# Banded attention by key groups, with the last two query tiles of its input product set between its first eight units

## What is computed

```python
def cd_mixer(u, w_in, w_out, conv_w, conv_b, w_a, b_a, w_x, b_x, lam, sinks):
    c_x, c_gate, d_q, d_k, d_v = _split(u @ w_in, CD_SIZES)      # 512, 512, 512, 128, 128 columns
    y_c = rg_lru_block(c_x, c_gate, conv_w, conv_b, w_a, b_a, w_x, b_x, lam)
    y_d = swa_sink_attention(d_q.reshape(bn, s_len, D_HEADS, D_HEAD_DIM), ...)
    return jnp.concatenate([y_c, y_d], axis=-1) @ w_out

def swa_sink_attention(q, k, v, sinks):      # 8 heads of 64, 2 key heads, 4 heads each
    ...
    s = jnp.einsum('bnqkgd,bnskd->bnkgqs', qc, kb).astype(F32) * (dh ** -0.5)
    s = jnp.where(valid[None, :, None, None, None, :], s, -jnp.inf)
    sink = ...
    p = jax.nn.softmax(jnp.concatenate([s, sink], axis=-1), axis=-1)[..., :-1]
    o = jnp.einsum('bnkgqs,bnskd->bnqkgd', p.astype(vb.dtype), vb)
```

## Time and profile before

| | |
|---|---|
| median of 3 runs | 2368.01 us (2366.35 to 2370.50) |
| the profiled execution | 2372.35 us, its span 2370.6 us |
| mean granted clock of TensorE | 0.992 of full |
| PE busy | 2324.5 us, 98% |
| DVE, ACT, POOL busy | 1646.2, 1026.0, 550.0 us (69%, 43%, 23%) |
| the chain that ended last | PE 90%, DVE 5%, ACT 3%, issue 1% |

### The profile page before, as it was taken

One profiled execution on the slowest core, in us unless ns is written; L12 is line 12 of the kernel. 1 busy time (PEld: TensorE's weight loads), 2 busy tenths in 40 slices (PEclk: granted clock), 3 DMA queues, 4 the chain that ended last, 5 costly groups with the idle time before them and its releaser, 6 DMA issues.

```text
span 2370.6 us, 33754 instructions
## 1 busy us (share of the span) xinstructions
PE 2324.5 (98%) x12906; PEld 1833.7 (77%) x12906; DVE 1646.2 (69%) x2657; ACT 1026.0 (43%) x1815; POOL 550.0 (23%) x510
## 2 busy tenths in 40 slices
PE   9999999999999999999999999989999999999998
PEld 6587778865587888888888867867878888888887
DVE  5388787887657977777655587456588677765557
ACT  5333335756634433333333444466343333333344
POOL 5025544323100243333320000000014333341000
PEclk9999999999999999999999999989999999999999
DMA  6121100010043455545696521101335445468663
GB/s 179 54 71 54 45 28 21 3 37 1 28 151 137 138 163 176 169 151 178 209 306 193 186 70 45 45 28 55 123 116 195 160 160 178 149 205 301 205 192 129
DMA packets 236271, 298.26 MB, mean 126 GB/s; under 512 B 13424, under 2 KB 175232, under 8 KB 227024
## 3 DMA queue, kind: packets, MB, share of 16 engines
q1 hardware_dynamic: 220848, 207.66, 28.4%
q0 software_dynamic: 15264, 88.45, 10.0%
HBM read 206.95 MB, written 88.60 MB: 125 GB/s over the span
## 4 chain that ended last, share of the span: by engine, by line
PE 90%; DVE 5%; ACT 3%; issue 1%; POOL 0%; DVEq 0%; ACTq 0%; POOLq 0%
PE ps L378 26%; PE ps L380 25%; PE ps L379 25%; PE ps L3228 2%; PE ps L3216 1%; PE ps L3248 1%; ACT d_p L1723 1%; PE ps L2555 1%; PE ps L2024 1%; DVE met L2326 1%; PE ps L2569 1%; PE ps L2564 1%; PE ps L1978 1%; PE ps L1537 1%; PE ps L2606 0%
## 5 line engine op out<-in xcount | busy, mean ns | idle before, releaser
L378 PE MATMUL ps<-uhi,whi 128*128 128x512 f32 x608 | 246.9, 406 | 7.6 <-DVE ulo L537 3.4
L378 PE MATMUL ps<-q_T,whi 128*128 128x512 f32 x640 | 249.1, 389 | 1.6 <-ACT upr L862 1.6
L380 PE MATMUL ps<-q_T,wlo 128*128 128x512 f32 x640 | 249.0, 389 | 0.0
L379 PE MATMUL ps<-q_T,whi 128*128 128x512 f32 x640 | 249.0, 389 | 0.0
L378 PE MATMUL ps<-q_B,whi 128*128 128x512 f32 x608 | 238.9, 393 | 2.4 <-DVE q_B L537 2.4
L378 PE MATMUL ps<-ahi,whi 128*128 128x512 f32 x616 | 240.4, 390 | 0.0
L380 PE MATMUL ps<-ahi,wlo 128*128 128x512 f32 x616 | 239.7, 389 | 0.0
L379 PE MATMUL ps<-alo,whi 128*128 128x512 f32 x616 | 239.7, 389 | 0.0
L380 PE MATMUL ps<-uhi,wlo 128*128 128x512 f32 x608 | 237.1, 390 | 0.0
L379 PE MATMUL ps<-ulo,whi 128*128 128x512 f32 x608 | 237.0, 390 | 0.0
L380 PE MATMUL ps<-q_B,wlo 128*128 128x512 f32 x608 | 236.7, 389 | 0.0
(11 more groups left out here) (485 smaller groups left out, 5001.4 us busy)
## 6 DMA issues: line engine op xcount, KB each, us to landing
wraw<-in_ffn_w_gate_dram SPq DMA_DIRECT2D x44, 512.0 KB, 5.5
wd<-in_ffn_w_down_dram POOLq DMA_DIRECT2D x22, 1024.0 KB, 7.3
w_sums<-wd POOLq DMA_DIRECT2D x22, 1024.0 KB, 4.9
wraw<-w_sums SPq DMA_DIRECT2D x40, 512.0 KB, 3.8
araw<-act_sums SPq DMA_DIRECT2D x40, 512.0 KB, 4.7
wraw<-in_ffn_w_down_dram SPq DMA_DIRECT2D x30, 512.0 KB, 5.9
araw<-acts SPq DMA_DIRECT2D x30, 512.0 KB, 6.7
wraw<-in_ab_w_in_dram SPq DMA_DIRECT2D x24, 512.0 KB, 3.8
```

The source lines that it names most:

```text
L378: nc.tensor.matmul(dst, wh, xh, start=start, stop=False, **kw)
L379: nc.tensor.matmul(dst, wh, xl, start=False, stop=False, **kw)
L380: return nc.tensor.matmul(dst, wl, xh, start=False, stop=stop, **kw)
```

## The change

The tiles are multiplied in another order: query tiles 0 and 1, keys, values, and then query tiles 2 and 3 (12 and 13 in the list). These two are no longer whole products ahead of the attention. Their 32 steps (three matmuls each: one channel piece, one half of the rows) are issued by `late_queries(pe, first_, end)` at given places: four before the transposes of the value tile, four after them, and 24 between the units 0 to 6. They use bank 0 for the first half of the rows and bank 1 for the second; `late_move(act, m)` copies each finished half (four copies of 512 columns in place of two of 1024).

The units go by groups: n is group n // 8, block n % 8, so that the first eight need query tiles 0 and 1 alone. The first eight share one pair of score banks (2 and 3), since 0 and 1 hold the late product: `scores(n + 1)` comes one unit ahead and waits for `bias(n)`. From unit 8 on the order is as before. The second weight tile of the output product is split inside the attention (ACT at n = 3, DVE at n = 4). `vrow`, `d_s`, `d_pt` and `d_p` have new places, since `uhi` and `ulo` are still read; POOL clears the first 64 columns of each `d_p` after `dk` is there.

```diff
-    order += [("cd", DQ0 + P * j) for j in range(6)]
+    order += [("cd", DQ0 + P * j) for j in (0, 1, 4, 5, 2, 3)]
...
-            for i in range(10, 13):
+            for i in range(10, 12):
                 pe.wait_ge(*after("dq_moved", i - 9))
                 gemm(pe, t[i], pair(i % 2), *u)
-            pe.wait_ge(*after("dq_moved", 4))
-            gemm(pe, t[13], pair(1), *u)
+            late_queries(pe, 0, 4)
             pe.wait_ge(*after("dv_copied", 1))
             for b in range(NB):
                 last = pe.transpose(pair(1)[:, b * P:(b + 1) * P], tmp[0][:, b * P:(b + 1) * P], ident[:, :])
             last.then_inc(S("dv_turned"), 1)
+            late_queries(pe, 4, 8)
+
+        def late_queries(pe, first_, end):
+
+            for s in range(first_, end):
+                i, h, k = 12 + s // 16, s // 8 % 2, s % 8
+                t = Tile(n_cd + i)
+                if s % 16 == 0:
+                    w_ready(pe, t)
+                if s == 0:
+                    pe.wait_ge(*after("dk_moved", 1))
+                if s in (16, 24):
+                    pe.wait_ge(*after("dq_moved", 3 + h))
+                last = three_pass(bank(h), whi[:, t.slot, k * P:(k + 1) * P], wlo[:, t.slot, k * P:(k + 1) * P],
+                                  uhi[:, k, rows_of(h)], ulo[:, k, rows_of(h)], k == 0, k == KT - 1)
+                if k == KT - 1:
+                    last.then_inc(S("w_used") if h else after("d_half", 0)[0], 1)
+
+        def late_move(act, m):
+
+            i, h = divmod(m, 2)
+            if h:
+                tile_done(act, Tile(n_cd + 12 + i))
+            else:
+                act.wait_ge(*after("d_half", i + 1))
+            act.activation(dq[:, 2 + i, rows_of(h)], bank(h), ACT.Copy).then_inc(S("dq_moved"), 1)
...
+        def d_bank(n):
+
+            return 2 if n < NB else 2 * (n % 2)
+
         def swa_pe(pe):
             def scores(n):
-                b, g = divmod(n, 2)
-                if n >= 2:
-                    pe.wait_ge(*after("d_biased", n - 1))
+                g, b = divmod(n, NB)
+                if n == NB:
+                    pe.wait_ge(*after("dq_moved", 6))
+                elif n:
+                    pe.wait_ge(*after("d_biased", n if n < NB else n - 1))
...
             scores(0)
-            scores(1)
-            for n in range(2 * NB):
+            ends = (8, 12, 16, 19, 23, 26, 29, 32)
+            for n in range(NB - 1):
+                scores(n + 1)
+                middle = ends[n + 1] if n == NB - 2 else ends[n] + 2
+                late_queries(pe, ends[n], middle)
+                turn(n)
+                late_queries(pe, middle, ends[n + 1])
+                if n:
+                    values(n - 1)
+            scores(NB)
+            for n in range(NB - 1, 2 * NB):
                 if n + 2 < 2 * NB:
                     scores(n + 2)
                 turn(n)
-                if n:
-                    values(n - 1)
+                values(n - 1)
             values(2 * NB - 1)
...
+            late_move(act, 0)
             soft(0)
             for n in range(2 * NB):
                 if n + 1 < 2 * NB:
                     soft(n + 1)
+                if n == 6:
+                    late_move(act, 3)
                 move(n)
                 if n:
                     result(n - 1)
+                if n == 1:
+                    late_move(act, 1)
+                if n == 3:
+                    w_high(act, Tile(first[("cd_out", 0)] + 1))
+                if n == 4:
+                    late_move(act, 2)
             result(2 * NB - 1)
...
                 norm(n)
+                if n == 4:
+                    w_low(dve, Tile(first[("cd_out", 0)] + 1))
```

More of the change, by code:

```diff
@@ L1414, in build_trunk @@
         dkx = at("dkx", [P, SEQ], 36 * KB)
[L1415 to L1418, removed]
+        vrow = at("vrow", [P, NB, P], 32 * KB)
+        d_s = [at(f"d_s{i}", [P, 4, 192], off * KB) for i, off in enumerate((204, 101))]
+        d_pt = [at(f"d_pt{i}", [P, 2, 4, P], off * KB) for i, off in enumerate((40, 116))]
+        d_p = [at(f"d_p{i}", [P, 4, 256], off * KB) for i, off in enumerate((112, 120))]
         wax = at("wax", [P, 8, P], 56 * KB)
@@ L1505, in d_prepare @@
             pool.dma_start(dkx[64:128, :], dk[0:64, :]).then_inc(S("dkx_landed"), 16)
-            pool.wait_ge(*after("dv_moved", 1))
-            pool.memset(d_p[:, :, :, 0:64], 0.0).then_inc(S("d_zero"), 1)
+            for i in range(2):
+                pool.memset(d_p[i][:, :, 0:64], 0.0).then_inc(S("d_zero"), 1)
         def c_halves(dve):
@@ L1567, in cd_act @@
             act.wait_ge(S("c_small"), C_SMALL)
-            for i in range(14):
-                if i + 2 < 14:
-                    w_high(act, t[i + 2])
+            for i in range(12):
+                w_high(act, t[i + 2])
                 j = i // 2
@@ L1617, in stt @@
                 return dve.scalar_tensor_tensor(out=out_, in0=in0, scalar=s, in1=in1, op0=a, op1=b)
-            for i in range(14):
-                if i + 2 < 14:
-                    w_low(dve, t[i + 2])
+            for i in range(12):
+                w_low(dve, t[i + 2])
                 j = i // 2
@@ L1673, in scores @@
                     part = slice(64 * odd, 64 * odd + 64)
-                    last = pe.matmul(bank(2 * (n % 2) + odd)[:, (h // 2) * 192 + k0:(h // 2) * 192 + 192],
+                    last = pe.matmul(bank(d_bank(n) + odd)[:, (h // 2) * 192 + k0:(h // 2) * 192 + 192],
                                      dq[part, j, b * P:(b + 1) * P],
@@ L1685, in turn @@
                     for h in range(4):
-                        last = pe.transpose(bank(4 + kt)[:, h * P:(h + 1) * P], d_p[:, n % 2, h, kt * P:(kt + 1) * P],
+                        last = pe.transpose(bank(4 + kt)[:, h * P:(h + 1) * P], d_p[n % 2][:, h, kt * P:(kt + 1) * P],
                                             ident[:, :])
@@ L3551, in _ @@
             cd_act(act)
-            high_two(act, ("cd_out", 0))
+            w_high(act, Tile(first[("cd_out", 0)]))
             swa_act(act)
@@ L3567, in _ @@
             cd_dve(dve)
-            low_two(dve, ("cd_out", 0))
+            w_low(dve, Tile(first[("cd_out", 0)]))
             swa_dve(dve)
```

38 lines of the change are left out of this document (19 added, 19 removed).

## The result

| | before | after |
|---|---|---|
| median of 12 runs each | 2367.46 us (2366.24 to 2371.05) | 2375.18 us (2371.68 to 2377.69) |
| ratio, 95% interval | | 1.0028 (1.0020 to 1.0035) |
| the profiled execution | 2372.35 us, span 2370.6 | 2377.18 us, span 2375.4 |
| mean granted clock | 0.992 | 0.995 |
| value tile's end, from the start | 1560.83 us | 1539.29 us |

A forecast was written before the change was run, and what follows sets the result against it. PE was taken as busy 98% of the span, with ACT full and PE nearly full in the steady attention. Terms sum to 87.4 us, less 21.8 is 65.6 against 61.64: +4.0 us, median 2372.0 us, range 2365 to 2379.

The forecast's parts named there:

- What is taken out: Input product: 32 steps of 0.68 us leave it, so the value tile ends 21.76 us earlier.
- (a): Value tile's end to the first scores: four steps, eight transposes, four steps, with the copies hidden; 6.5 us.
- (b): Units 0 and 1, up to the start of scores(2), with narrow work for unit 0; 7.3 us.
- (c): Iterations 1 to 5: a serial chain of 3.9 us from scores to turn, PE still for 1.7 us each; 34.3 us.
- (d): Iteration 6: three steps ahead of its turn and none behind; 6.0 us.
- (e): From scores(8) through turn(7) and eight units to the output product; 32.5 us.
- (f): Product matmuls behind plain f32 ones, seven times outside the waits, cost 0.11 us more each; 0.8 us.
- the clock falls: Rival, chance 0.10: a new wait in the first units lowers PE's clock, adding 6 us; 2378 us.
- The chain covered: Rival, chance 0.08: probabilities are ready when the steps end, so PE never waits before turns; -5.5 us, 2362.5 us.
- Covered in part: Rival, chance 0.07: earlier scores or bias save 0.6 us an iteration, -3.6 us in all; 2368.4 us.
- the same in another way: Cross-check of the attention stretch: 15 of 61.6 us were waiting or half clock before, 19 after, 9.5 in new waits.

The follow-up runs named there:

- e1: The changed kernel with all steps of a unit ahead of its turn and none behind; median 2367.22 us, ratio 0.9995 to the kernel before.
- e2: The changed kernel with no step ahead of turns 0 to 6, all behind them; median 2393.26 us, ratio 1.0100 to the kernel before.
- e3: The changed kernel with norm(n) ahead of bias(n + 1) on DVE for units 0 to 6; median 2367.74 us, ratio 0.9989 to the kernel before.
- e6: The changed kernel run again unedited, beside the kernel before on the same chip; median 2374.07 us, ratio 1.0020.
- e5: The kernel before with nine product steps nobody reads, placed where PE waited at the handover; median 2367.87 us, ratio 1.0000.
- e9: The changed kernel with small unread matmuls in the waits before turns 7, 14, 15 and the output product; median 2371.12 us, ratio 1.0010 to the kernel before.
- e4: The changed kernel with all 32 steps ahead of the first scores and scores two units ahead; median 2364.28 us, ratio 0.9986 to the kernel before.
- e7: The kernel before run again unedited for a second profile; 2366.58 us in one profile.
- e10: e4 with both output tiles split ahead of the attention and unread matmuls before turns 14, 15 and the output product; median 2365.57 us, ratio 0.9984 to the kernel before.

## Why the prediction was right, and where it was short

**The direction and most of the size**: +4.0 us predicted; +4.8 by the profiles, +7.7 by the medians, +5.1 to +6.1 group against group. The number 2372.0 is 3.2 us under the median of 2375.18, which lies within the stated range of 2365 to 2379 and just outside the 2369.5 to 2375 that the forecast gave itself. That +4.0 and +4.8 are so near is in part luck: the stage gave +3.1, and a fall of the clock that the sum did not have gave the rest.

**What is taken out**, 32 steps of 0.68 us: the value tile ends 21.54 us earlier, as said. The product's matmuls keep their distance of 0.23 us among the units (1568.14 less 1567.91), so the lower figure of the Trainium skill, page TensorE: Matmul & The Clock Gate, section Back-to-back issue gap, does not describe this stream here either (0.23 us measured against about 0.13), and giving it no chance was right.

**(a) and (b)**, 6.5 + 7.3 = 13.8 us to the start of scores(2): 1553.18 - 1539.29 = 13.9.

**(c)**, the heart: 3.9 us from scores to turn were predicted and 3.90 measured. An iteration was put at 6.7 or 7.4 us and took 6.64 (1584.58 - 1577.95) or 7.33. From scores(2) to scores(7) the trace has 1587.32 - 1553.18 = 34.1 us where the sum had 34.3. e1, e2 and e3 show that this chain is the cause. The wait was put at 1.7 us and recorded as 1.39. This is the same event: the sum counted a step as 0.68 us from start to start, while the record counts idle time from the end of the last matmul, 0.17 us later, and the dearer first matmul of the two steps takes another 0.1.

**(d)**: 6.0 predicted from scores(7) to scores(8), 1593.26 - 1587.32 = 5.9 measured, with a wait of 0.71 us at turn 6 for the 1.0 said.

**(e)**: 3.4 us to turn(7), 23.8 for eight units, 5.34 to the output product; measured 3.43, 23.76 (1620.45 - 1596.69) and 5.33.

**(f)**: a product matmul behind plain f32 ones costs 0.31 to 0.33 us to the next start, so about 0.1 more each, as taken. But the parts (a) to (e), each measured from start to start, add up to 13.89 + 34.14 + 5.94 + 32.52 = 86.49 with it inside, where the sum had 86.6 without it. A turn with a step behind it took 0.85 us (1571.47 - 1570.62) and not the 1.03 of the sum, which pays for the dearer matmul. So the 0.8 us of (f) is most of what the sum had too much: **87.4 us predicted, 86.5 measured**. The waits, 9.5 us predicted, are 5 x 1.39 + 0.71 = 7.7 by the record.

**What the sum lacked** is a price of the clock. The forecast had it at full through the stage and gave "the clock falls" 0.10, with the waits of 1.7 us in units 1 to 5 as its place. There the clock held, in both profiles of the changed kernel. But the prediction never priced two other places: turn 7, which has no step ahead of it and waits 2.06 us, and the output product, which had waited 2.03 us at full clock before and was taken over unchanged. In the profile after, the second cost 1.5 us; in e6 both fell. The wait at turn 7 is new, and its fall cost 1.6 us in e6 and nothing in after. The fall at the output product can come in the kernel before too, as e5 has it. e9 puts the average of what fills recover at both at about 1 us. So the sum was 0.9 us high in the stage and lacked this term.

**The rivals.** The chain covered, -5.5 us: it did not come true in the changed kernel. e3 makes it true by DVE's order and nets -3.9 in the stage; its profile has a fall at turn 7, worth 1.6 us, and without it the net is the -5.5 that the rival was priced at. Covered in part: not seen, no iteration is shorter than the chain allows. The clock: right as a mechanism, as e2 shows at 2.98 us of waiting and e4 at 1.80, but it did not come at 1.39.

**The sense of "the same in another way"**, 15 us of the old stage as waiting or half clock, was too generous: e5 and e7 show that the half clock in it cost nothing up to turn 1 and 0.5 us at most behind it.

## What to carry to other kernels

When work is put between two links of a chain, count the chain from the first link (here scores to turn, 3.9 us) and not the work alone: up to the chain's slack the work is free, and behind its end it is paid in full, so all of it belongs ahead of the waiting instruction (e1) or in front of the whole chain (e4). When a prefetch goes from two units ahead to one, look at every in-order queue that serves both units: swapping two calls on DVE made the stage 7 us shorter (e3). Where the clock differs from one execution to the next, compare group with group, and take in every execution of a group; two medians of the same kernel were 2.6 us apart here, nearly half of the effect.

## What the runs showed of the hardware that was not expected

- TensorE fell to 1.2 GHz behind single waits of 2.03 to 2.06 us in some executions and kept 2.4 GHz in others, at the same place of the same program (turn 7: 1.00 in the profile after, 0.57 in e6; behind the wait of 2.03 us at the output product: seven of ten profiles fell). Behind a wait of 1.80 us it fell too (e4, 0.57). The waits of the units 0 to 6 in the changed kernel, 0.71 to 1.39 us with 5.9 to 7.3 us from turn to turn, did not do it in three profiles; six of 2.98 us, behind one of 2.71, did again and again (0.67 to 0.95 in e2). A fall costs 1.5 to 1.6 us at turn 7 and at the output product, where PE is the bound, and nothing up to turn 1 of the kernel before, where it is not.
- Whether it falls at 520 to 545 us moves everything behind by 5.6 us, in the same kernel, from one execution to the next. What decides it stays open; no edit here touches it.
- The last 19 us of the span come at a mean clock of 0.88 to 0.91 or of 0.82 to 0.83, and take 0.6 to 0.8 us more at the lower one (e10 apart, with 19.25 us at 0.91).
- In e9 and e10 the four calls of `fill` (128 x 128 weight, 256 columns, f32) took 1.99 us and stood in the wait of 2 us at the output product; the clock was at 1.00 there in both. Two profiles do not show that the fills held it, since it stayed at 1.00 in three of ten without them, but the executions of e9 together are about 1 us nearer to the kernel before.
